# Wide products in the last expert rows, two early rows in front of the picks, tile-by-tile products in the first mixers' stage

## The reference

```python
s = einsum('bthpd,hpkd->bthpk', q, sub_keys)             # 8 heads, 2 halves, 128 keys
s_top, i_top = lax.top_k(s, 16)
best, pos = lax.top_k(cand, 16)                          # of the 16 x 16 sums
gates = softmax(best)
a = gelu(einsum('nd,nkd->nk', x, u_emb[experts]))
y = einsum('nk,nkd->nd', gates * a, v_emb[experts])
```

## Time and profile before

| | |
|---|---|
| runs | 1583.4, 1586.64, 1588.95 us, median 1586.64 |
| profiled execution | 1584.84 us, its span 1583.0 us |
| mean granted TensorE clock | 0.985 of full |
| TensorE, VectorE, ScalarE, GpSimd busy | 96%, 74%, 54%, 22% |
| largest groups | expert and dense products of 256 columns (L508, L514), v products (L2966) |
| moved by DMA | 272 MB, 172 GB/s on average |

### The profile page before, as it was taken

One profiled execution on the slowest core, in us unless ns is written; L12 is line 12 of the kernel. 1 busy time (PEld: TensorE's weight loads), 2 busy tenths in 40 slices (PEclk: granted clock), 3 DMA queues, 4 the chain that ended last, 5 costly groups with the idle time before them and its releaser, 6 DMA issues.

```text
span 1583.0 us, 32051 instructions
## 1 busy us (share of the span) xinstructions
PE 1526.1 (96%) x10720; PEld 1379.4 (87%) x10720; DVE 1178.0 (74%) x2312; ACT 851.2 (54%) x1573; POOL 354.2 (22%) x265
## 2 busy tenths in 40 slices
PE   9899998999999899899999899999999999999997
PEld 7788987999887786698999899988888899999996
DVE  5778676798848678455499778789999777777776
ACT  5564454666548654565455465554444555444455
POOL 3234332011100331222068765630000000000000
PEclk9889999999999999999999999999999999999999
DMA  8323244555565720254656555467777656655654
GB/s 287 119 94 120 81 139 154 153 186 184 187 187 173 253 76 1 80 187 147 194 161 217 183 176 156 152 199 240 242 240 241 210 187 186 185 185 185 187 185 158
DMA packets 89289, 272.22 MB, mean 172 GB/s; under 512 B 9984, under 2 KB 27520, under 8 KB 88832
## 3 DMA queue, kind: packets, MB, share of 16 engines
q1 hardware_dynamic: 65520, 238.06, 47.1%
q10 hardware_dynamic: 23696, 33.17, 6.6%
HBM read 259.13 MB, written 12.06 MB: 171 GB/s over the span
## 4 chain that ended last, share of the span: by engine, by line
PE 82%; DVE 13%; ACT 2%; issue 2%; DMA 1%; POOL 0%; DVEq 0%; ACTq 0%; SPq 0%
PE ps_chunk L508 22%; PE ps_misc L2966 22%; PE ps_chunk L514 11%; PE ps_misc L300 6%; PE ps_chunk L1931 4%; PE ps_chunk L501 3%; PE ps_chunk L520 3%; PE ps_misc L2901 3%; PE ps_chunk L300 2%; PE ps_chunk L524 2%; PE ps_chunk L529 1%; PE ps_misc L1010 1%; DVE mixers_arena L2680 1%; DVE mixers_arena L2679 1%; DVE mixers_arena L2676 1%
## 5 line engine op out<-in xcount | busy, mean ns | idle before, releaser
L425 ACT ACTIVATE w_hi<-raw 128x512 fp32r<-128x512 f32 (+2 forms) x898 | 546.6, 627 | 489.1 <-PE ps_chunk L514 193.7
L432 DVE TENSOR_TENSOR w_lo<-raw,w_hi 128x512 fp32r<-128x512 f32 x663 | 488.6, 755 | 247.1 <-ACT w_hi L425 238.0
L508 PE MATMUL ps_chunk<-x_hi,w_hi 128*128 128x256 f32 x1792 | 459.0, 288 | 2.0 <-ACT w_hi L425 1.6
L508 PE MATMUL ps_chunk<-x_lo,w_hi 128*128 128x256 f32 x1792 | 452.3, 285 | 0.0
L432 POOL TENSOR_TENSOR w_lo<-raw,w_hi 128x512 fp32r<-128x512 f32 (+2 forms) x237 | 311.3, 1329 | 518.8 <-ACT w_hi L425 454.8
L508 PEld LDWEIGHTS ps_chunk<-x_hi,w_hi 128*128 128x128 f32 x1792 | 345.8, 193 | 6.2 <-ACT w_hi L425 2.2
L508 PEld LDWEIGHTS ps_chunk<-x_lo,w_hi 128*128 128x128 f32 x1792 | 346.6, 193 | 2.9 <-issue 0.5
L514 PE MATMUL ps_chunk<-x_hi,w_lo 128*128 128x256 f32 x1792 | 290.0, 285 | 1.9 <-DVE w_lo L432 0.9
L514 PEld LDWEIGHTS ps_chunk<-x_hi,w_lo 128*128 128x128 f32 x1792 | 248.4, 193 | 3.2 <-POOL w_lo L432 2.0
L2966 PE MATMUL ps_misc<-w_hi,hid_hi 128*128 128x512 f32 x508 | 198.3, 390 | 1.6 <-issue 1.6
L2966 PE MATMUL ps_misc<-w_hi,hid_lo 128*128 128x512 f32 x508 | 198.8, 391 | 0.0
(11 more groups left out here) (423 smaller groups left out, 1818.3 us busy)
## 6 DMA issues: line engine op xcount, KB each, us to landing
raw<-in_stream SPq DMA_DIRECT2D x452, 512.0 KB, 3.7
early_rows<-row ACTq DMA_DIRECT2D x68, 128.0 KB, 2.3
row<-early_rows ACTq DMA_DIRECT2D x66, 128.0 KB, 3.1
memory_kv<-mixers_arena ACTq DMA_DIRECT2D x4, 512.0 KB, 5.0
mixers_arena<-in_cmp_w ACTq DMA_DIRECT2D x1, 2048.0 KB, 10.2
mixers_arena<-memory_kv ACTq DMA_DIRECT2D x4, 512.0 KB, 6.4
mixers_arena<-in_consts ACTq DMA_DIRECT2D x1, 1729.0 KB, 10.8
row<-in_rows ACTq DMA_DIRECT2D x3, 512.0 KB, 7.6
```

Source lines behind the costliest of these rows:

```text
L425: e.activation(w_hi[q % 2][:, s], raw[q][:, s], ACT.Copy).then_inc(made, 1)
L432: e.tensor_tensor(w_lo[q % 2][:, s], raw[q][:, s], w_hi[q % 2][:, s].bitcast(F32), ALU.subtract).then_inc(made, 1)
L508: e.matmul(o, w[0][:, k * P:(k + 1) * P], x[:, k, :], start=k == 0 and x is x_hi, stop=False, skip_group_check=True)
```

## The change

There are three parts. **Last rows.** `x_hi` and `x_lo` become the two halves of one buffer `x_both`, so one product of 512 columns (`wide_products`) multiplies a tile of high weights by both; high x high lands in the first 256 columns of the bank, high x low in the next 256. The low weights are multiplied by `x_hi` alone (`narrow_products`). ScalarE copies the second 256 columns to SBUF (`cross_out`), VectorE adds them to the first (`summed`), and ScalarE's Gelu works in place on the sum. TensorE's queue is now wide j, v row j-2, narrow j. u units take `w_hi[0]` and `w_lo[0]` and v units the other two, as before, but each kind has counts of its own; VectorE raises the low counts for the unused units, which nobody splits any more. **Early rows.** 34 rows stand in front of the transposes and two behind them, and ScalarE splits the row after next. **Order of products.** Up to the end of the first weave feature units use `tile_by_tile` and token units `run`; later the high-first forms stand, but for the first half unit of every token chunk, which uses `run`.

```diff
--- before.py
+++ after.py
...
-        x_hi, x_lo = sb("x_hi", [P, KD, T], F32R), sb("x_lo", [P, KD, T], F32R)
+        x_both = sb("x_both", [P, 2, KD, T], F32R)
+        x_hi, x_lo = x_both[:, 0, :, :], x_both[:, 1, :, :]
...
-                        if q == 0 and part == 0 and n:
-                            e.wait_ge(*left[t])
...
-            pe.quiet(by_tiles if not token_major else run if x_made or by_token else by_weights)
+            def tile_by_tile(e):
+
+                e.wait_ge(made, u + 1)
+                if q % 2 == 0 and part == 0 and some == 0 and n:
+                    e.wait_ge(*left[q // 2])
+                for k in range(4 * part + 2 * some, 4 * part + 2 * some + 2):
+                    last = product3(e, ps[:, q * T:(q + 1) * T], [a[:, k * P:(k + 1) * P] for a in w],
+                                    [x[:, k, :] for x in (x_hi, x_lo)], k == 0, k == KD - 1)
+                if some:
+                    last.then_inc(used_up, 1)
+
+            if not token_major:
+                pe.quiet(by_tiles if high_first[0] else tile_by_tile)
+            else:
+                pe.quiet(run if x_made or by_token or (q == 0 and part == 0) or not high_first[0] else by_weights)
...
+        high_first[0] = True
...
-        def ahead(e, q, chunk, i):
-
-            split_hi(e, (q + 1) % 4, chunk + (chunk_early + (q + 1) // 4))
+        def ahead(e, q, chunk):
+
+            split_hi(e, (q + 2) % 4, chunk + (chunk_early + (q + 2) // 4))
...
-                def four(c):
-                    for q in range(UNITS):
+                def some(c, rows=range(UNITS)):
+                    for q in rows:
                         bank_left(e, c * 4 + q)
                         for part in range(2):
                             u_products(e, q % 2, q % 2, c * 4 + (u_early + q), range(4 * part, 4 * part + 4), part)
                 if last:
-                    four(EARLY_SELECT // 4 - 1)
+                    some(EARLY_SELECT // 4 - 1, range(2, UNITS))
                     return
-                four(0)
+                some(0)
                 with e.Fori(1, EARLY_SELECT // 4 - 1) as c:
-                    four(c)
+                    some(c)
+                some(EARLY_SELECT // 4 - 1, range(2))
 
             def activation_rows(e, begin, end):
                 def four(c):
                     for q in range(UNITS):
-                        ahead(e, q, c, None)
+                        ahead(e, q, c)
                         early_gelu(e, q, c * 4 + q)
+                if begin == 0:
+                    split_hi(e, 1, chunk_early)
                 four(begin // 4)
...
-                            split_hi(e, q, c + v_chunk)
+                            if not (begin and q == 1):
+                                split_hi(e, q, c + v_chunk)
...
+            cross = [xn[:, 1, 512 + s * T:512 + (s + 1) * T] for s in range(2)]
...
-                def u_row(b, j):
-                    bank_left(e, j + EARLY)
-                    for part in range(2):
-                        u_products(e, b, 0, j * 2 + u0, range(4 * part, 4 * part + 4), part)
+
+                def wide_products(b, j):
+                    if later(j, 2):
+                        e.wait_ge(s_summed, j - 1)
+                    else:
+                        e.wait_ge(s_gel, EARLY)
+                    for half in range(2):
+                        e.wait_ge(u_high[half], j + 1)
+                        for k in range(4 * half, 4 * half + 4):
+                            last = e.matmul(ps_chunk[b][:, 0:2 * T], w_hi[0][:, k * P:(k + 1) * P], x_both[:, :, k, :],
+                                            start=k == 0, stop=False, skip_group_check=True)
+                        last.then_inc(u_wide[half], 1)
+
+                def narrow_products(b, j):
+                    for half in range(2):
+                        e.wait_ge(low_made[half], j * 2 + (u0 + 1))
+                        for k in range(4 * half, 4 * half + 4):
+                            last = e.matmul(ps_chunk[b][:, 0:T], w_lo[0][:, k * P:(k + 1) * P], x_hi[:, k, :],
+                                            start=False, stop=k == KD - 1, skip_group_check=True)
+                        last.then_inc(u_done[half], 1)
 
                 def v_row(b, j):
-                    v_unit(e, b, 1, j + EARLY, j * 2 + (u0 + 3))
-
-                u_row(0, 0)
-                unused(e, u0 + 1)
-                u_row(1, 1)
-                v_row(0, 0)
+                    e.wait_ge(s_hid, j + (EARLY + 1))
+                    for half in range(2):
+                        e.wait_ge(low_made[half], j * 2 + (u0 + 4))
+                        for t in range(TT):
+                            last = product3(e, ps_misc[:, 2 * t + half, :],
+                                            [x[:, b, t * P:(t + 1) * P] for x in (hid_hi, hid_lo)],
+                                            [a[1][:, halves[half]] for a in (w_hi, w_lo)], False, False)
+                        last.then_inc(v_done[half], 1)
+
+                for j in range(2):
+                    wide_products(j, j)
+                    narrow_products(j, j)
                 with e.Fori(1, rest // 2) as m:
                     for b in range(2):
-                        u_row(b, m * 2 + b)
-                        v_row(1 - b, m * 2 + (b - 1))
-                unused(e, u0 + 2 * rest)
-                v_last(e, 1, 1, P - 1, u0 + 2 * rest + 1)
...
+                        wide_products(b, m * 2 + b)
+                        v_row(b, m * 2 + (b - 2))
+                        narrow_products(b, m * 2 + b)
+                v_row(0, rest - 2)
+                v_last(e, 1, 1, P - 1)
+
+            def activation_rest(e):
+
+                def u_highs(j, q, n):
+                    e.wait_ge(s_w[q], n * 16 + 16)
+                    for half in range(2):
+                        if later(j, 1):
+                            e.wait_ge(u_wide[half], j)
+                            e.wait_ge(low_made[half], j * 2 + (u0 - 1))
+                        else:
+                            e.wait_ge((s_use1, s_use)[half], u0 - 1)
+                        e.activation(w_hi[0][:, halves[half]], raw[q][:, halves[half]], ACT.Copy).then_inc(u_high[half], 1)
+
+                def v_highs(j, q, n):
+                    e.wait_ge(s_w[q], n * 16 + 16)
+                    for half in range(2):
+                        if later(j, 1):
+                            e.wait_ge(v_done[half], j)
+                        else:
+                            e.wait_ge((s_use1, s_use)[half], u0)
+                        e.activation(w_hi[1][:, halves[half]], raw[q][:, halves[half]], ACT.Copy).then_inc(v_high[half], 1)
+
+                def cross_out(b, j):
+                    e.wait_ge(s_u_done, j + 1)
+                    if later(j, 2):
+                        e.wait_ge(s_summed, j - 1)
+                    e.activation(cross[b], ps_chunk[b][:, T:2 * T], ACT.Copy).then_inc(s_cross, 1)
+
+                def gelu(b, j):
+                    e.wait_ge(s_summed, j + 1)
+                    e.activation(gel[b], gel[b], ACT.Gelu_apprx_tanh).then_inc(s_gel, 1)
+
+                def row(b, j, q, n, nn):
+                    cross_out(1 - b, j - 1)
+                    gelu(1 - b, j - 1)
+                    u_highs(j + 1, (q + 2) % 4, nn)
+                    v_highs(j - 1, q + 1, n)
...
+                    row(0, m * 2, 0, m + first, m + first)
+                    row(1, m * 2 + 1, 2, m + first, m + (first + 1))
...
+                def u_lows(j, q, some=(0, 1)):
+                    for half in some:
+                        e.wait_ge(u_high[half], j + 1)
+                        if later(j, 1):
+                            e.wait_ge(u_done[half], j)
+                        e.tensor_tensor(w_lo[0][:, halves[half]], raw[q][:, halves[half]],
+                                        w_hi[0][:, halves[half]].bitcast(F32), ALU.subtract).then_inc(low_made[half], 1)
...
+                def unused(q, n):
+                    e.wait_ge(s_w[q], n * 16 + 16)
+                    for half in range(2):
+                        e.wait_ge(low_made[half], n * UNITS + q)
+                        e.sem_inc(low_made[half], 1)
+
+                def summed(b, j):
+                    e.wait_ge(s_u_done, j + 1)
+                    e.wait_ge(s_cross, j + 1)
+                    e.wait_ge(s_own, EARLY + j - 1 if isinstance(j, int) and j > 1 else EARLY if isinstance(j, int) else
+                              j + (EARLY - 1))
+                    e.tensor_tensor(gel[b], ps_chunk[b][:, 0:T], cross[b], ALU.add).then_inc(s_summed, 1)
+
+                def gated(b, j):
+                    e.wait_ge(s_gel, j + (EARLY + 1))
+                    gate_row(e, b, b, j + EARLY)
+
+                def row(b, j, q):
+                    u_lows(j, q, (0,))
+                    summed(1 - b, j - 1)
+                    u_lows(j, q, (1,))
+                    gated(1 - b, j - 1)
```

(1 more changed line is left out.)

82 lines of the change are left out of this document (46 added, 36 removed).

## The result

| | before | changed |
|---|---|---|
| median of four executions each | 1585.02 us | 1564.03 us |
| range | 1577.22 to 1588.95 | 1562.59 to 1566.48 |
| the profiled execution: time, span | 1584.84, 1583.0 | 1562.93, 1561.1 |
| granted clock, mean | 0.985 | 0.989 |

A forecast was written before the change was run, and what follows sets the result against it. The prediction took TensorE, busy 96% of the span, as the bound. Its terms, −5.3 − 0.4 − 5.7 − 1.7 + 0.9 − 0.2 = −12.4 us, gave 1574.2 us from a median of 1586.64, range 1569 to 1580.5.

The forecast's parts named there:

- Wide products, −5.3: Last 60 rows: 8 products of 512 columns replace 16 of 256, saving 0.011 us a pair, 5.3 us in all.
- Start of the last stage, −0.4: Last stage's start: TensorE's 0.41 us around semaphore bookkeeping for an unused unit moves to VectorE, 0.4 us less.
- End, "no change": End of the last stage: the last v row again waits about 0.4 us, taken as no change.
- Does TensorE stay the bound: Last stage: VectorE needs 4.5 us and ScalarE 3.2 against a row of 5.53, so the new work costs nothing.
- Two early rows, −5.7, and clock, −1.7: At the picks: two rows fill TensorE's 5.16 us wait, 5.7 us less; full clock behind it, 1.7 us less.
- First mixers' stage, +0.9 and −0.2: New product order there: a late low half delays the chain, 0.9 us more; one token-unit wait goes, 0.2 us less.
- (b): Rival: first stage gets cheaper because the half clock of 83.1 to 93.3 us stays away; 1569.1 us, chance 0.08.
- In the later stages only each chunk's first half unit changes; nothing: Product order in the stages after the first mixers' stage: claimed to cost or save nothing.
- (a): Rival: first stage gets dearer by one more half-clock stretch, 6.8 us long, costing 3.4; 1577.6 us, chance 0.10.
- (c): Rival: in the last stage the wide products save next to nothing; 1579.5 us, chance 0.09.
- (d): Rival: the two early rows do not fit before the transposes, as GpSimd or ScalarE feeds late; 1579.9 us, chance 0.05.
- (e): Rival: the last stage's row becomes a slower chain on VectorE and ScalarE, 5.85 us a row; 1593.7 us, chance 0.04.

The follow-up runs named there:

- e5: The changed kernel run again unchanged: mean 1568.5 us against 1584.6 for the kernel before on the same chip, ratio 0.9896.
- e12: The changed kernel run a third time, unchanged: mean 1569.2 us against 1585.1 for the kernel before on the same chip, ratio 0.9900.
- e16: The changed kernel run a fourth time, unchanged: median 1570.02 us against 1582.05 for the kernel before on the same chip, ratio 0.9921.
- e11: The changed kernel with one early row instead of two in front of the picks' transposes: mean 1570.6 us.

## Why the forecast was wrong

- **The sum as such.** The change is worth 16 us by its deterministic part (15.8 behind 785 us, in four profiles out of four) and 16.1, 15.9 and 13.1 us by the means of e5, e12 and e16 on their chips. The forecast had 12.4. The 21 us of the first comparison (19.8 by the means) hold some 4 to 5 us more that belong to these few executions: the early rows start at 785.5, 791.8, 787.9 and 787.4 us in the changed kernel's four profiles, at 791.6 and 785.1 in the two of before. The step that failed first is the one from the profile to the range: the forecast took the half clock in the profile of before as fixed and gave no spread to its first 785 us, which moved by 6 us between two executions of one program; its own spread of 1571 to 1578 held bounds of costs alone. The second is the sum behind 785 us, 13.1 us where 15.8 were measured (the terms below). The base of 1586.64 us, a median of three, was 1.6 above that of the four executions compared. For the first 785 us the forecast had 0.7 us more; taking 15.8 from the three repeated comparisons leaves 0.3 and 0.1 us less and 2.7 more. So that total was not refuted, but it was right by luck: both orders' effects, below, were forecast wrongly and work against each other. The means of the repeats, 1568.5 and 1569.2 twice, lie at the lower edge of the range.
- **Wide products, −5.3: mis-sized.** I took 0.229 us, the mean of a row's v products. That mean holds a 0.03 us start-up behind narrow products, which moves to the wide ones and isn't bought twice. The right price was the 0.2267 us of the long run, which I had as a bound: 0.0133 x 480 = 6.4, measured 6.34. The other bound was wrong for these products: 0.2267 and 0.120 us leave a fixed part of 13.3 ns over the columns at 2.4 GHz. The 2.5 ns of the Trainium skill ("TensorE: Matmul & The Clock Gate", section "Back-to-back issue gap") are given there for the gap of a product by itself, and the measurement does not bear them out for this stream.
- **Start of the last stage, −0.4: right, and somewhat small.** The first wide product starts at 1221.79, the end of the v rows, and no wait follows. Before, the eight products behind the 0.41 us wait also took 1.19 us where such eight take 0.96, which makes 0.64 us in all:

```profile
1239.01 0.41 issue
1239.41 1.19 PE ps_chunk L508 x8
```

- **End, "no change": wrong, −0.5.** The chain of before has 0.40 us of "issue" in front of the last v row, whose six products then take 1.64 us:

```profile
1571.23 0.40 issue
1571.63 1.64 PE ps_misc L2985 x6
```

  In the changed kernel the last v row (L3004) stands right behind the one ahead and takes 1.50, so its hidden values were ready in that one's 2.75 us:

```profile
1547.12 2.75 PE ps_misc L502 x12
1549.87 1.50 PE ps_misc L3004 x6
```

  With the wide products (6.34) and the start (0.64) these 0.54 us make 7.52 of the 7.53.
- **Does TensorE stay the bound: right.** The sum took 0.417 us against my 0.476.
- **Two early rows, −5.7, and clock, −1.7: right.** The transposes start 0.40 us earlier relative to the early rows, two rows (5.76) are gone behind them, the transposes save 1.03 and the first eight products 0.58: 7.77. The Trainium skill, "TensorE: Matmul & The Clock Gate", section "HAM oscillation — how this bites in real kernels", says that idle gaps let the clock drop for what follows; e11's trace agrees, with half clock behind 2.8 us of idle time.
- **Wait for the early v rows, 0: it shrank from 1.6 to 1.0 us,** which no term had.
- **First mixers' stage, +0.9 and −0.2: wrong in sign.** The delay I followed did not come: the mixer's step at 41.28 starts at 41.5 us on average with the old order (six profiles) and with the new (nine; in e5, after 6.8 us of half clock at its start, 43.8). What I did not follow is where the moved work goes. With the new feature order the clock is full at 58 us in ten profiles of eleven, and at 82 us in all of them: 4.3 us net, with the longer half clock at 48 us or the new one behind 71 us counted in. In five of the six profiles with the old order there is half clock at both. This is the rival (b), with the half clock at 83 us as its place and 5.1 as its price; it got 0.08, on the argument that VectorE leaves TensorE idle anyway. It still does, but in shorter pieces: from 66 to 100 us the longest idle time is 2.6 us in all seven profiles with the old feature order, in front of the products at 83 us, and 1.8 us in all eleven with the new. That the shorter pieces keep the clock is argued and not tried.
- **"In the later stages only each chunk's first half unit changes; nothing": wrong.** At 515 to 528 us the first half unit of a chunk is fed by a late transfer, and the low half's 1.3 us stands in its way: 2.7 us on average, with half clock somewhere from 515 to 535 us in all nine profiles with the new order, against four of nine with the old.
- The rivals (a), (c), (d) and (e) did not happen: the first stage did not get dearer, the width paid, the rows fitted, VectorE kept up.

## What to carry to other kernels

Profile the kernel before twice before you price a part in which the clock changes: its stretches moved the same 785 us by 6 us here, half of what was forecast for the whole change, while everything behind was the same to 0.2 us. Price an instruction from a long run of its kind, not from a row in which it follows another kind. When an order is changed for one stage, look at each place where the same function starts on freshly loaded data: here high products first were worth most where a transfer landed late.

## What the runs showed of the hardware

- fp32r products of 512 and 256 columns follow each other in 226.7 and 120 ns at full clock, 13.3 ns over the columns at 2.4 GHz. Behind 256-column products the first five of 512 took 233, 236, 228, 232 and 231 ns.
- The half clock comes and goes between executions of one program, mostly at the same places. At 58 us it was there after 1.9 to 3.0 us of idle TensorE, but four profiles stood idle 2.0 us there and kept the full clock. Two products of 512 columns and the twelve behind them took 2.6 us at full clock and up to 4.7.
- VectorE's product of two 128x512 SBUF tiles at 57 us (L1560 before) took 1.75 us in the twelve profiles where GpSimd was making a low half when it started, and 0.69 in the six where it was not. The Trainium skill, "VectorE: DVE Perf Modes", section "Two Vector instructions with no wait between them", has VectorE's second SBUF read interface shared with GpSimd; the trace agrees. That this is the cause was not tried by itself.
